# Seven block products for eight in three quarters of the second feed-forward product

## What is computed

```python
mix = sigmoid(ga) * (ya @ w_branch_a) + sigmoid(gb) * (yb @ w_branch_b)
h = h + rmsnorm(mix @ w_out, norm_attn_post)
u = rmsnorm(h, norm_ff_pre)                        # (256, 2048)
f = square(relu(u @ w_ff1)) @ w_ff2                # w_ff1 (2048, 8192), w_ff2 (8192, 2048)
h = h + rmsnorm(f, norm_ff_post)
```

## Time and profile before

| | |
|---|---|
| median of 3 runs | 1331.21 us (1330.93 to 1331.58) |
| span of the profiled execution | 1329.9 us |
| TensorE matmul busy | 1321.3 us, 99% |
| VectorE busy | 805.7 us, 61% |
| ScalarE busy | 630.0 us, 47% |
| DMA | 252.6 MB, mean 190 GB/s |
| granted TensorE clock | full speed in all 40 slices |

### The profile page before, as it was taken

One profiled execution on the slowest core, in us unless ns is written; L12 is line 12 of the kernel. 1 busy time (PEld: TensorE's weight loads), 2 busy tenths in 40 slices (PEclk: granted clock), 3 DMA queues, 4 the chain that ended last, 5 costly groups with the idle time before them and its releaser, 6 DMA issues.

```text
span 1329.9 us, 18980 instructions
## 1 busy us (share of the span) xinstructions
PE 1321.3 (99%) x7070; PEld 1131.4 (85%) x7070; DVE 805.7 (61%) x1129; ACT 630.0 (47%) x904; POOL 50.5 (4%) x93
## 2 busy tenths in 40 slices
PE   9999999999999999999999999999999999999998
PEld 7889999888888888889988888888888888888886
DVE  7766565687875555557765455565456555466554
ACT  7454453556664444444744344443444443344442
POOL 1222110000000000000100000000000000000000
PEclk9999999999999999999999999999999999999999
DMA  9766555655566667675766666666666656666663
GB/s 313 203 185 169 170 161 148 167 166 159 167 191 190 188 189 223 225 231 161 248 189 193 192 192 189 190 190 192 195 192 187 189 196 193 190 190 190 191 191 109
DMA packets 147879, 252.55 MB, mean 190 GB/s; under 512 B 8659, under 2 KB 45935, under 8 KB 147420
## 3 DMA queue, kind: packets, MB, share of 16 engines
q1 hardware_dynamic: 143888, 241.40, 60.4%
q0 software_dynamic: 2160, 4.74, 1.8%
q10 hardware_dynamic: 1756, 5.36, 1.2%
HBM read 249.29 MB, written 2.17 MB: 189 GB/s over the span
## 4 chain that ended last, share of the span: by engine, by line
PE 99%; DMA 0%; DVE 0%; ACT 0%; SPq 0%; issue 0%; ACTq 0%
PE bank L1380 18%; PE bank L1382 17%; PE bank L1381 17%; PE bank L1690 16%; PE bank L1693 9%; PE bank L1426 4%; PE bank L1414 3%; PE bank L1415 3%; PE bank L1413 3%; PE bank L1428 2%; PE bank L1714 1%; PE bank L1717 1%; PE bank L1505 1%; PE bank L1504 1%; PE bank L1368 1%; DMA raw<-in_w_in 0%
## 5 line engine op out<-in xcount | busy, mean ns | idle before, releaser
L818 DVE TENSOR_TENSOR w_lo<-raw,w_hi 128x1024 fp32r<-128x1024 f32 (+1 forms) x456 | 549.9, 1214 | 407.6 <-ACT w_hi L442 406.1
L442 ACT ACTIVATE w_hi<-raw 128x1024 fp32r<-128x1024 f32 (+1 forms) x456 | 474.7, 1050 | 484.4 <-DMA raw<-in_w_ff 362.4
L1690 PE MATMUL bank<-f_hl,w_hi 128*128 128x512 f32 x960 | 229.7, 391 | 0.0
L1690 PEld LDWEIGHTS bank<-f_hl,w_hi 128*128 128x128 f32 x960 | 176.4, 188 | 34.1
L1380 PE MATMUL bank<-w_hi,hid_hi 128*128 128x512 f32 x512 | 199.2, 389 | 0.0
L1382 PE MATMUL bank<-w_hi,hid_lo 128*128 128x512 f32 x512 | 199.2, 389 | 0.0
L1381 PE MATMUL bank<-w_lo,hid_hi 128*128 128x512 f32 x512 | 199.2, 389 | 0.0
L1693 PEld LDWEIGHTS bank<-f_hl,w_lo 128*128 128x128 f32 x960 | 123.1, 191 | 4.7
L1693 PE MATMUL bank<-f_hl,w_lo 128*128 128x256 f32 x960 | 124.5, 283 | 0.0
L1382 PEld LDWEIGHTS bank<-w_hi,hid_lo 128*128 128x128 f32 x512 | 96.1, 188 | 20.0
L1381 PEld LDWEIGHTS bank<-w_lo,hid_hi 128*128 128x128 f32 x512 | 96.1, 188 | 19.9
(11 more groups left out here) (252 smaller groups left out, 1504.1 us busy)
## 6 DMA issues: line engine op xcount, KB each, us to landing
raw<-in_w_ff SPq DMA_DIRECT2D x256, 512.0 KB, 3.8
raw<-in_w_in SPq DMA_DIRECT2D x128, 512.0 KB, 3.7
raw<-in_w_out SPq DMA_DIRECT2D x32, 512.0 KB, 4.6
raw<-in_w_branch_b SPq DMA_DIRECT2D x16, 512.0 KB, 3.7
raw<-in_w_branch_a SPq DMA_DIRECT2D x16, 512.0 KB, 3.8
xt<-in_turned_x SPq DMA_DIRECT2D x8, 272.0 KB, 5.8
raw<-in_w_in SPq DMA_DIRECT2D x8, 256.0 KB, 5.8
bias<-bias_table POOLq DMA_DIRECT2D x8, 256.0 KB, 4.6
```

The costliest lines, as they stand in the source:

```text
L442: act.activation(w_hi[:, u, :, 0:width], raw[:, u, :, 0:width], ACT.Copy).then_inc(hi_ready, 1)
L818: dve.tensor_tensor(w_lo[:, u, :, 0:width], raw[:, u, :, 0:width], w_hi[:, u, :, 0:width].bitcast(F32), ALU.subtract).then_inc(lo_ready, 1)
L1690: ins = pe.matmul(acc[g][:], w_hi[:, u, k, cols], f_hl[:, kt, :], start=kt == 0, stop=kt == KT - 1)
```

## The change

**Products.** In quarters 0 to 2 the second product goes over two halves of 1024 columns (c = 0, 1), and in each over the four groups of four k-tiles that one ff1 chunk left (j = 0 to 3). The first two k-tiles of a group, the two token blocks and the two 512-column blocks make a 2 x 2 by 2 x 2 block product, which is now computed with seven block products instead of eight (Strassen's scheme in Winograd's form): item "W", 7 x 3 matmuls. The other two k-tiles are multiplied as before, one item "S" each: four block products, 12 matmuls. `ORDER` is W, S, S for each group. Four of the seven products sum in banks 0 to 3 over all groups of a column half and are added to a new SBUF tile `pacc`; the three others go straight into banks 4 to 7 with the S items, and those banks are added to `facc`. The last quarter computes ff2 as before.

**Joining.** In ff1 chunks 1 and 2 of the last quarter VectorE joins `pacc` and `facc` by eight additions of 1024 elements (`join`); at chunk 3 ScalarE multiplies `facc` by `rstd2`, which the additions of quarters 0 to 2 no longer do.

**Weights.** A W item has one DMA of 1 MB into the first four of seven tiles of `b_raw`; VectorE computes the other three combinations, and a fourth over one that was loaded, in three dependent subtractions; then high and low parts are made in two steps, "first" (three tiles) and "rest" (four). There are two such buffers. An S item has one DMA of 512 KB; there are three buffers. They lie over `raw`, `w_lo` and `w_hi`, and the third S buffer lies over the scratch of the hidden tile (`work`), so its load waits for `hid_lo_ready` of chunk 3. `SPLITS` is the order of ScalarE and VectorE: first(0), rest(0), S0, first(1), S1, rest(1), S2, first(2), S3, rest(2), S4 and so on; the hidden steps of chunk 3 stand behind S0 and behind first(1).

**Hidden tile.** VectorE adds four steps of 128 elements to each ff1 chunk of these quarters (three more token combinations); the hidden tile's parts have 11 blocks of 128 for 8.

**Else.** The SBUF layout is rearranged, GpSimd also clears `pacc`, and the load of `norm_ff_post` moves from the first to the last quarter. The core of the diff, in this order: the items; SP's loads; ScalarE behind its four chunks; VectorE in `activate_hidden`, in `split_item` and behind its four chunks; TensorE in `multiply_seven`:

```diff
+SEVEN = (0, 1, 2, 3)
+        if _j in SEVEN:
+            ORDER += [("W", _c, _j), ("S", _c, 4 * _j + 2), ("S", _c, 4 * _j + 3)]
...
+            def load_ff2(q):
+                before = uses_before(q)
+                load_s(q, 0, None)
+                load_w(q, 0, before + 24 + 4)
+                load_w(q, 1, before + 24 + 7)
+                load_s(q, 1, before + 24 + 8)
+                sp.wait_ge(hid_lo_ready, 4 + q * 4)
+                load_s(q, 2, None)
+                for i, it in enumerate(ORDER):
+                    n = (W_AT if it[0] == "W" else S_AT).index(i)
+                    if it[0] == "W" and n + 2 < N_W:
+                        load_w(q, n + 2, before + 32 + i + 1)
+                    elif it[0] == "S" and n + 3 < N_S:
+                        load_s(q, n + 3, before + 32 + i + 1)
...
+            def quarter(q, first=False):
+                head = SPLITS.index(("S", 0)) + 1
+                for it in SPLITS[:head]:
+                    split_item(q, *it)
+                act.wait_ge(hid_lo_ready, 3 + q * 4)
+                copy_hidden(q, 3)
+                split_item(q, *SPLITS[head])
+                keep_hidden(q, 3, False)
+                for it in SPLITS[head + 1:]:
+                    split_item(q, *it)
+                split_next(q, *range(LEAD))
...
+                square.then_inc(hid_part, 1)
+                dve.wait_ge(hid_part, n + 1)
+                dve.tensor_tensor(work[:, 8, :], work[:, 3, :], work[:, 1, :], ALU.add).then_inc(hid_part, 1)
+                dve.wait_ge(hid_part, n + 2)
+                dve.tensor_tensor(work[:, 3, :], work[:, 2, :], work[:, 3, :], ALU.subtract)
+                dve.tensor_tensor(work[:, 9, :], work[:, 8, :], work[:, 2, :], ALU.subtract).then_inc(hid_part, 1)
+                dve.wait_ge(hid_part, n + 3)
+                dve.tensor_tensor(work[:, 10, :], work[:, 0, :], work[:, 9, :], ALU.subtract).then_inc(hid_ready, 1)
...
+            def split_item(q, kind, n):
+                if kind == "first":
+                    dve.wait_ge(b_landed[i], 16 * (n // 2 + 1) + q * (16 * N_W // 2))
+                    dve.tensor_tensor(raw_b[:, 4:2:-1, :], raw_b[:, 3:0:-2, :], raw_b[:, 2:4, :], ALU.subtract)\
+                       .then_inc(b_part, 1)
+                    dve.wait_ge(b_part, part + 1)
+                    dve.tensor_tensor(raw_b[:, 5, :], raw_b[:, 1, :], raw_b[:, 4, :], ALU.subtract).then_inc(b_part, 1)
+                    dve.wait_ge(b_part, part + 2)
+                    dve.tensor_tensor(raw_b[:, 6, :], raw_b[:, 0, :], raw_b[:, 5, :], ALU.subtract).then_inc(b_ready, 1)
+                    dve.wait_ge(b_ready, n + 1 + q * N_W)
+                    dve.wait_ge(hi_ready, split_no(q, kind, n))
+                    dve.tensor_tensor(lo[:, 0:3, :], raw_b[:, 0:3, :], hi[:, 0:3, :].bitcast(F32), ALU.subtract)\
+                       .then_inc(lo_ready, 1)
+                elif kind == "rest":
+                    dve.wait_ge(hi_ready, split_no(q, kind, n))
+                    dve.tensor_tensor(lo[:, 3:7, :], raw_b[:, 3:7, :], hi[:, 3:7, :].bitcast(F32), ALU.subtract)\
+                       .then_inc(lo_ready, 1)
...
+                head = SPLITS.index(("S", 0)) + 1
+                for it in SPLITS[:head]:
+                    split_item(q, *it)
+                activate_hidden(q, 3, False)
+                split_item(q, *SPLITS[head])
+                keep_hidden(q, 3, False)
+                for it in SPLITS[head + 1:]:
+                    split_item(q, *it)
+                    if it == ("rest", N_W // 2):
+                        add_p(q, 0)
+                    if it == ("S", N_S // 2):
+                        add_x(q, 0)
...
+                for n, (tokens, weights, to) in enumerate(((2, 2, 0), (8, 4, 1), (3, 3, 2), (9, 5, 3), (0, 0, 4), (10, 1, 5),
+                                                           (1, 6, 6))):
+                    if n == 1:
+                        pe.wait_ge(lo_ready, split_no(q, "rest", k))
+                    if opens and c == 0 and n in (0, 4):
+                        pe.wait_ge(hid_summed, 12 + n + 16 * q)
+                    if opens and c == 1:
+                        pe.wait_ge(acc_free, base + n + 1)
+                    ins = three(bank[to][:], hid7_hi[:, j, tokens, :], hid7_lo[:, j, tokens, :], w_h[:, weights, :],
+                                w_l[:, weights, :], opens, closes and n < 4)
```

More of the change, by code:

```diff
@@ L215, in hybrid_block @@
         dcol = sb("dcol", [P, 1])
-        sink_bc = sb("sink_bc", [P, HB])
         sc = sb("sc", [P, 96])
@@ L363, in _, with load_ff1 @@
                          8 * C_OUT + u - 7 + n * 8)
-            with sp.Fori(0, QUARTERS) as q:
-                for j in range(4):
-                    for u in range(UNITS):
[L367 to L372, removed]
+            def load_ff1(q, j, u, free):
+                load(u, w_ff1, slice(u * 256, u * 256 + 256), bass.ds(q * D + j * CW, CW), free)
@@ L747, in quarter, with split_next @@
+            def split_next(q, *units):
+                for u in units:
+                    split_hi(u, C_FF + 4 + q * 4)
+            def quarter(q, first=False):
+                for j in range(4):
                     if first and j == 0:
@@ L787, in _ @@
                 quarter(q)
-            quarter(QUARTERS - 1, last=True)
+            for j in range(4):
+                chunk_ff1(QUARTERS - 1, j, last=True)
+            for u in range(LEAD):
+                split_hi(u, C_FF + 4 + (QUARTERS - 1) * 4)
+            for j in range(4):
+                chunk_ff2(j)
             for b in range(BLOCKS):
@@ L1761, in _, with chunk_ff1 @@
-            quarter(0, first=True)
-            for q in range(1, QUARTERS - 1):
-                quarter(q)
-            quarter(QUARTERS - 1, last=True)
+            def chunk_ff1(q, j, first=False):
+                if first and j == 0:
+                    first_chunk()
+                    return
+                if first and j == 1:
+                    pe.wait_ge(turned_lo, T_F)
+                elif j < 2:
+                    pe.wait_ge(acc_free, 2 * C_FF + 16 * q - (0 if j else 4))
+                else:
+                    pe.wait_ge(hid_summed, 4 * (j - 1) + q * 16)
+                for u in range(UNITS):
+                    multiply_hidden(8 * (C_FF + j) + q * STEP, u, [bank[4 * (j % 2) + g] for g in range(4)])
@@ L1768 @@
+            for q in range(QUARTERS - 1):
+                quarter(q, q == 0)
+            for j in range(4):
+                chunk_ff1(QUARTERS - 1, j)
+            for j in range(4):
+                chunk_ff2(j)
 _INS = ["x", "meta_tokens", "rel_bias", "w_in", "w_branch_a", "w_branch_b", "w_out", "lambda_q1", "lambda_k1",
```

467 lines of the change are left out of this document (338 added, 129 removed).

## The result

| | before | after |
|---|---|---|
| median | 1331.24 us (4 runs) | 1351.59 us (4 runs, 1351.29 to 1355.35) |
| ratio | | 1.0159, interval 1.0145 to 1.0174 |
| span of the profiled execution | 1329.9 us | 1349.6 us |

The kernel became 1.6% slower: 20.4 us by the medians, 19.7 by the spans. The prediction said slower, by 11 us; the time lies 0.6 us above its range.

The account below looks back on a forecast made before the run. TensorE, 99% busy, bounds the kernel. Per ff2 stage 81.6 us of matmuls plus waits of 6.0, 1.1 and 2.0 make 90.7 for 87.0; three times +3.7 is +11.0, so 1342 us, range 1333 to 1351.

Parts of the forecast that it names:

- VectorE's chain at the head of a stage: Start of each ff2 stage: 19.0 us of VectorE work after W0's landing, against 13.0 that TensorE leaves; 6.0 us late.
- W0's other four: Head of an ff2 stage: W0's last four low parts are wanted at 0.7 us and ready at 1.5.
- S1's wait: Head of an ff2 stage: TensorE stands 4.7 us because W1's parts and the hidden low part precede S1's low part.
- S9 in the middle: Middle of an ff2 stage: S9's low part is ready at 57.3 us, wanted at 55.4; 2.0 us lost.
- S3: After the head of an ff2 stage: S3 is ready at 24.8 us, TensorE stands 1.1 us.
- Landing of 1 MB: A W item's load lands 5.2 us after issue; bounds 3.8 and 7.3, skill's estimate 4.4.
- cover suffices: Rival for the ff2 stages: VectorE's head chain is 15.3 us or less, no net loss; 1315 to 1330 us; chance 0.10.
- about nothing: Rival for the ff2 stages: fast landing and dearly counted order or overlap, stalls 5 to 6 us; 1329 to 1333; chance 0.07.
- slow loads: Rival for the W loads: 1 MB lands as late as the broadcast, 7.3 us; 1361 us; chance 0.06.
- Rival (c): Long standstills in ff2 stages: TensorE's clock falls, 1.5 us lost each, three times 4.6; 1347 us; chance 0.17.
- the next quarter's first units are ready at its start: Start of the next quarter's ff1: its first units' loads cause no lateness; costed at nothing.
- Hidden at no cost: Last quarter's eight joins (10 us unhidden), ScalarE's scaling (4 us), GpSimd's memset and the moved gain load add no time.

Follow-up runs that it names:

- The first edit: Changed kernel, with quarter 0's loads of chunk 0's units issued in order 0 to 7 again: 1345.39 us, ratio 1.0105.
- group 1 plain: Changed kernel with quarter 0's loads in order 0 to 7 and W1 and W5 multiplied by eight block products, 366 matmuls per stage: 1334.73 us, ratio 1.0021.
- The last two kernels with group 1 plain: On the kernel with group 1 plain, W2's load and first part go earlier: 1324.19 us; with W0's load two units earlier as well: 1321.20 us.
- the three kernels whose clock stays at 1.00 in the stages: Groups 1 to 3 by eight products: 1331.04 us; group 1 plain with W2's load and first part earlier: 1324.19; with W0's load earlier too: 1321.20.

## Why the prediction was right or wrong

**Right: the direction and its cause.** The prediction said that VectorE's chain at the head of a stage takes more than the cover, and that its order sets S1's start. It measured as computed, piece by piece. VectorE of after at quarter 1's head, stage start 891.95:

```profile
886.23 1.23 DVE L1498 TENSOR_TENSOR b_raw<-b_raw 128x1024 f32<-128x1024 f32 x1 [6.10 <-DMA b_raw<-in_w_ff]
...
890.90 2.29 DVE L1510 TENSOR_TENSOR b_lo<-b_raw,b_hi 128x2048 fp32r<-128x2048 f32 x1
893.11 1.22 DVE L1514 TENSOR_TENSOR s_lo<-s_raw,s_hi 128x1024 fp32r<-128x1024 f32 x1
...
902.48 1.62 DVE L1469 TENSOR_TENSOR hid_lo<-work,hid_hi 128x1408 fp32r<-128x1408 f32 x1
904.02 1.22 DVE L1514 TENSOR_TENSOR s_lo<-s_raw,s_hi 128x1024 fp32r<-128x1024 f32 x1
```

From the landing at 886.23 (forecast -5.5, here -5.7) to the end of S1's low part at 905.24 it is 19.0 us, with no gap over 0.13 us: the forecast's number. 2048 elements take 2.29 us, as estimated, and 1408 take 1.62.

**Step by step, quarter 1's stage of 92.26 us.** Matmuls 81.6, as forecast. W0's other four: 0.7 for 0.8, of which 0.45 is idle time and the rest the slower restart (the two matmuls behind a wait start some 0.3 us late in sum). Banks: 0.4 for 0.4. S1's wait from the timeline (905.38 - 900.39 - 0.23): 4.8 for 4.7. S9 in the middle (1.71 us idle, 2.0 by the spacing of the matmuls): 2.0 for 2.0; in quarter 0 its wait was 1.3. S3: 0 for 1.1. Slow S1: 2.7 for 0. Sum 92.2.

**Landing of 1 MB:** 5.1 us in after, 5.2 forecast; the estimate of 4.4 from the Trainium skill, "DMA: Bandwidth & Descriptors" (Anatomy of one DMA), and the fast and slow ends did not come. The rivals "cover suffices", "about nothing" and "slow loads" are excluded by it and by the chain above.

```profile
b_raw<-in_w_ff SPq DMA_DIRECT2D x24, 1024.0 KB, 5.1
```

Two steps failed, and either alone would have left the time inside the range: without the 4.8 us of the second it is 1346.8, without the 3.8 of the first 1347.8.

**Wrong, first: the clock was kept as a rival and not in the sum.** The sum put the clock's fall at nothing. Rival (c) had its condition right, a standstill of 4.7 us longer than any in the trace, and it had a row at the end of before where the clock falls some 3 us after the last matmul. I gave it 0.17 and priced it at 1.5 us per stage. It came in all three stages and cost 2.5 to 2.7, because the level stays low for 5.1 to 5.6 us of work and not for 3. A part of that is paid out of S3's wait of 1.1, which fell under the slow S1 and is back as soon as S1 is fast (1.0 to 1.1 us with twenty extra matmuls). Net 1.0 to 1.5 us per stage, 3.8 in all: (91.74 + 92.26 + 92.06) - 3 x 90.74.

**Wrong, second and larger: a step costed at nothing.** The prediction said "the next quarter's first units are ready at its start", and costed next quarter's loads at nothing. That holds for quarters 1 to 3, whose ff1 stages are 89.06 us. It was not asked of quarter 0, whose loads go through the same sorted function with no stage before them. The first edit shows the place: 5.4 us of that part, 4.8 at its end (TensorE reached it 0.6 us earlier). With 3.8 from the clock it makes the 8.6 us between forecast and span (1349.6 - 1340.9 = 8.7).

**Hidden at no cost** were, as said, the joins, the scaling and the clears: the last quarter takes 184.3 us in both kernels.

**What the experiments add to the forecast's theory.** Where VectorE has nothing to spare, exchanging two of its steps moves the wait (S1 earlier: nothing gained); where it has, it removes it (S9 earlier: 2.8 us). Each wait removed at the head left the next one: S1, then S3, then W0's. The gain appeared with the first two gone (1324 with 366 matmuls, for 1331 before and 1345 with 360), and the third gave 3 us more. Of the 12.2 us that 54 fewer matmuls are worth, 10.2 arrive.

Open is what decides whether the clock falls behind a given gap: it held behind the 1.7 us for S9 in quarter 1 of after and fell behind 1.8 us for the same item in quarter 0 with twenty extra matmuls; with group 1 plain it held behind 1.8 us for S3 in quarter 0 and fell behind 2.0 in quarter 1. With S1 ahead of W1 it fell behind 1.83 us for S9 in quarter 1 and held behind 1.83 us for S9 in quarter 2, so the length of a gap alone does not decide. The last two kernels with group 1 plain avoid the question, they do not answer it.

## What to carry to other kernels

Trading TensorE work for VectorE work is decided at the place where the buffers start empty, not by the average: add up the chain from the first landing to the first item that stands behind another item's preparation, and compare it with the work that TensorE has in hand. In these kernels a standstill of TensorE of about 2 us or more was mostly followed by slow matmuls that lost another 1.3 to 3 us. Count it with them, and do not expect to win by shortening it halfway. When a load order is changed for the steady case, follow every queue through the first pass too.

## What the runs showed of the hardware

- The granted clock fell to the lower level behind or within standstills of 3.2 to 4.6 us every time; behind some of 1.8 to 2.4 us and not behind others (the longest that it held behind is 2.2 us, with GpSimd's combinations), and behind 2.2 and 1.4 us with three matmuls between. It was low for 3.4 us in some of these heads and for 6.8 in others of the same kernel. The runs of one kernel differ with it: those of the first kernel with group 1 plain spread over 6 us, those of the three kernels whose clock stays at 1.00 in the stages over 0.9 to 1.6.
- fp32 subtractions on GpSimd and VectorE at the same time often slow each other: 1024 elements took 2.39 to 4.32 us on GpSimd and 1.21 to 3.44 on VectorE. With GpSimd's combinations the kernel took 1362.94 us, for 1345.39 with VectorE's (the order of the parts differed too).
- A 1 MB load on SP's queue lands 5.1 us after its issue, a 512 KB load 3.9 us (medians in after).
